# Sample tokens of a streaming trunk layer: two heads on the 128 partitions in both attentions, and two squares of x moved to VectorE

## The chip, the cores and the metric

The kernel runs on one core of one Trainium2 chip. The metric is the time of one execution on the device in microseconds (us), as a median of runs. Matrix products run on TensorE (PE in the profile, its weight loads PEld), elementwise work on VectorE (DVE), ScalarE (ACT) and GpSimd (POOL). SyncE (SP) only issues transfers. All times are in us unless marked ns.

## The reference

One inference step of one layer of a hybrid trunk, for 256 prompt tokens and 64 sample tokens of width 1024:

```python
h = rms_norm(x, p['norm_mix'])
proj = h @ p['w_in']                       # gated delta rule, and queries, latent and rope key of the first attention
o_gdn, s_new = gated_delta_rule(...)       # 4 heads, chunks of 64 tokens
o_mla = block_causal_attention(q * (QK_DIM ** -0.5), k_mla, v_mla, q_pos, k_pos)   # 4 heads, 128 nope + 64 rope
x = x + concatenate([o_gdn, o_mla]) @ p['w_out']

h = rms_norm(x, p['norm_mem'])
sm = einsum('bqhd,bkhd->bhqk', qm, mem_k)  # 4 heads over 256 memory tokens
om = einsum('bhqk,bkhd->bqhd', softmax(sm), mem_v)
x = x + om @ p['w_mo']

h = rms_norm(x, p['norm_ffn'])
x = x + moe_ffn(h, ...)                    # top 4 of 32 experts, w_gu (1024 x 2048), w_down (1024 x 1024) each
```

All of it is in float32. The prompt's first attention is causal by chunks over its own tokens; the 64 sample tokens see 256 cached and 64 own keys, 320 in all.

## The kernel before

Tokens lie in three blocks of rows: two of 128 prompt tokens and one of 64 sample tokens (`TB = 3`, `DEC = 64`). Each engine runs a program of its own; the five are tied together by counting semaphores. The order of the work up to the first attention is a list written out by hand (`CHAIN`). A float32 product is two pairs of weight load and MATMUL in the trace, so counts of such instructions are twice the counts of products. Nearly all products are recorded at L1075 (`mm`), transposes at L1078 (`tr`), ScalarE's activations at L630 (`run`), VectorE's at L1861, L1865, L1866 (`tt`, `ts`).

**Start.** The rows of x are loaded by `ld_x0`, `ld_x1`, `ld_x2`. ScalarE squares the two prompt blocks with an accumulated sum (`x0_sq`, `x1_sq`). VectorE squares the sample rows in two instructions, a product (L1861) and a reduction at L1925 (`x2_sq`). When all three sums stand, ScalarE takes the logarithm and the exponential (`x_logs`, `x_rstd`), VectorE makes diagonals of the result, and TensorE spreads them over the columns before the first projection.

**The two attentions** (`attention`, once in the program of TensorE, ScalarE and VectorE each) go over a list of units, one for each pair of block and head. There are 12: units 0 to 3 are block 0, 4 to 7 block 1, 8 to 11 the sample rows. Step n of TensorE does the scores of unit n, the transposes of the probabilities of unit n-2 and the product with V of unit n-3. VectorE takes the maximum of unit n, scales the probabilities of unit n-1 by the reciprocal of their sum (L2224) and copies out unit n-3 (L2230, `att_o`). ScalarE takes the exponential of unit n and copies the transposes of unit n-2 out of PSUM. A sample unit has 64 rows, thus 64 of 128 partitions. Two banks hold scores, two the transposes, two the results.

Other work is placed between the steps by step number. In the first attention (`mla`), from step 8 on, TensorE adds pieces of the output projection (`GO_AT`: two at step 8, one at each step 9 to 14), and from step 7 on ScalarE scales one eighth of a weight matrix a step (`WQ_AT`). In the second (`mem`), steps 0 to 5 bring x back to rows, `MO_AT` places the four halves of the output projection of blocks 0 and 1 (`mem_out`) at steps 8, 9, 12 and 13, and `X3T_AT` the transposes of block 0 at step 11. `mem_out` waits for the copies of its block's units (`att_o`). ScalarE's square of block 0 (`square_rows(0)`, L1011) is done at step `X3T_AT`, its first bf16 part at `X3T_AT + 3`. Then come the router, the transposes of the other blocks and the projection of the sample rows (`mem_out_pair`, which writes the two halves of the columns to two halves of the partitions).

**Experts.** Each expert takes six tiles of 2 MB, loaded through nine slots. The first nine loads are written out: slots 2 and 3 after the convolution state is stored, 4 and 5 after the first attention, 8, 0, 1, 6 and 7 as their places come free, the last when the router has done its third block. From then on a slot is loaded again (`refill`, L545, or L553 for the last ones) when the tile before it in that slot is used. The loop over experts starts with the gather of expert 0's rows, which needs the router's choice.

Of the kernel before, what the change touches and what calls it, by code (L numbers as in the profile page):

```python
# [88 lines left out]
def trunk_kernel(nc, x_prompt, x_sample, cache_kv_latent, cache_k_rope, state_gdn, state_conv, cache_mem_k,  # L89
# [5 lines left out]
    with ctx:  # L95
# [5 lines left out]
        def sem(name):  # L101
# [9 lines left out]
            "scalar": ["x0_sq", "x1_sq", "x_logs", "x_rstd", "gains_ready", "conv_ready", "bexp_ready", "egc_ready", "kpe_ev"],  # L111
            "vector": ["x2_sq", "diag0", "diag2", "diag1", "rbc_ev", "upad_ready", "state0", "sp_abs", "g_ready", "g2_ready", "gcum_ready", "diff_ready", "dec_ready",
# [16 lines left out]
        ATT = {"mla": 0, "mem": H * TB}  # L129
# [200 lines left out]
        def half(s):  # L330
            return slice(CH * s, CH * s + CH)
# [17 lines left out]
        for b in range(TB):  # L349
            for h in range(H):  # L350
                rows = P if b < 2 else DEC
                qs = slice(b * P, b * P + rows)
                ks = slice(0, (b + 1) * P) if b < 2 else slice(SEQ, NKEY)
                vs = [vk[:, i, h * P:(h + 1) * P] for i in range(b + 1)] if b < 2 else \
                    [vk[:, 2, h * P:(h + 1) * P], vk[:, 3, h * P:(h + 1) * P], vk[0:DEC, 4, h * P:(h + 1) * P]]
                mla_units.append((rows, [(qTn[:, h, qs], kT[:, h, ks]), (qTr[:, h, qs], kpeT[:, ks])],
                                  ks.stop - ks.start, b < 2, vs, hT[:, H + h, qs]))
        for b in range(TB):
            for h in range(H):
                rows = P if b < 2 else DEC  # L360
                qs = slice(b * P, b * P + rows)
                km, vm = (km_p, vm_p) if b < 2 else (km_s, vm_s)
                mem_units.append((rows, [(qmT[:, h, qs], km[:, h, :])], NMEM, False,
                                  [vm[:, i, h * P:(h + 1) * P] for i in range(2)], om[:, h, qs]))
# [218 lines left out]
        def _(pool):  # L583
# [23 lines left out]
            for b in range(TB):  # L607
                if b == 1:
                    pool.wait_ge(sem("att_pv"), ATT["mem"] + H * TB)
# [18 lines left out]
        def _(act):  # L628
# [319 lines left out]
            def attention(tag, units, scale, between):  # L948

                for n in range(len(units) + 3):  # L950
                    between(n)
                    if n < len(units):
                        rows, terms, nkeys, masked, vs, out = units[n]
# [3 lines left out]
                        run(prob[0:rows, n % 2, 0:nkeys], PS[n % 2][0:rows, 0:nkeys], ACT.Exp, scale=scale,  # L957
                            bias=amx[0:rows, n % 2:n % 2 + 1], accum_out=asum[0:rows, n % 2:n % 2 + 1])\
                            .then_inc(sem("att_ex"), 1)
                    if 2 <= n <= len(units) + 1:  # L960
                        rows, terms, nkeys, masked, vs, out = units[n - 2]
# [4 lines left out]
                        if vs[-1].shape[0] == P:  # L966
                            m = run(probT[:, u, 0:len(vs) * P].rearrange("p (t q) -> p t q", q=P)[:, :, 0:rows],
                                    PS[2 + u][:, 0:len(vs) * P].rearrange("p (t q) -> p t q", q=P)[:, :, 0:rows])
                        else:
                            for t, v in enumerate(vs):  # L970
                                m = run(probT[0:v.shape[0], u, t * P:t * P + rows], PS[2 + u][0:v.shape[0], t * P:t * P + rows])
                        m.then_inc(sem("att_pt"), 1)

            def conv_states_and_keys(n):
# [8 lines left out]
                if WQ_AT <= n < WQ_AT + KD:  # L983
                    k = n - WQ_AT
# [40 lines left out]
            def first_block(n):  # L1025
# [4 lines left out]
                if n == X3T_AT + 3:  # L1030
                    part(0, 0)
# [41 lines left out]
        def _(pe):  # L1073
# [429 lines left out]
            def attention(tag, units, between, behind=None):  # L1503


                for n in range(len(units) + 3):
                    between(n)
                    if n < len(units):
                        rows, terms, nkeys, masked, vs, out = units[n]
# [4 lines left out]
                        for t, (q, k) in enumerate(terms):  # L1514
                            m = mm(PS[n % 2][0:rows, 0:nkeys], q, k, t == 0, t == len(terms) - 1)
                        m.then_inc(sem("att_s"), 1)
                    if 2 <= n <= len(units) + 1:
                        rows, terms, nkeys, masked, vs, out = units[n - 2]
# [4 lines left out]
                        for t, v in enumerate(vs):  # L1523
                            kr = v.shape[0]
                            m = tr(PS[2 + u][0:kr, t * P:t * P + rows], prob[0:rows, u, t * P:t * P + kr])
                        m.then_inc(sem("att_tr"), 1)
                    if n >= 3:
                        rows, terms, nkeys, masked, vs, out = units[n - 3]
# [4 lines left out]
                        for t, v in enumerate(vs):  # L1533
                            kr = v.shape[0]
                            m = mm(PS[4 + u][:, 0:rows], v, probT[0:kr, u, t * P:t * P + rows], t == 0, t == len(vs) - 1)
# [6 lines left out]
            def conv_states_and_keys(n):  # L1542
# [19 lines left out]
                for g in {GO_AT: (0, 1)}.get(n, (n - GO_AT + 1,) if n > GO_AT else ()):  # L1562
# [958 lines left out]
```

## Time and profile before

| | |
|---|---|
| median of 3 runs | 1306.26 (1306.18 to 1307.25) |
| time of the profiled execution | 1307.44 |
| its span, first to last instruction | 1305.5 |
| TensorE busy | 1268.4, 97% of the span |
| VectorE busy | 466.9, 36% |
| ScalarE busy | 209.8, 16% |
| GpSimd busy | 21.7, 2% |
| moved by DMA | 439.20 MB, mean 336 GB/s |
| mean granted TensorE clock | 0.997 |

The span is what the trace shows; the time of the same execution is 1.9 longer. The share of busy time is a mean over stages that have different limits, and ends of MATMULs are modelled, so times of products are better taken from start to start. A row of the timeline gives the start, the busy time of a run of like instructions, engine, line, operation, out<-in, and in brackets the idle time of the engine before it and what ended it.

### The profile page before, as it was taken

The numbers are of one execution on the slowest core, as the hardware profiler recorded it, in microseconds if no ns is written. First come the engines' busy times: TensorE is split into PE (matmuls) and PEld (weight loads), VectorE is DVE, ScalarE is ACT, GpSimd is POOL, SyncE is SP. The second block draws the span as 40 slices with busy tenths as digits, with TensorE's granted clock in tenths as the row PEclk, the third lists the DMA queues.
The fourth block names the chain that finished last, engine by engine and source line by source line (L and its number), as shares of the span: only waits on it lengthen the run. The fifth ranks groups of instructions, "written<-read, shape, count | busy, mean of one in ns | idle before, by whom it ended". The sixth has DMA issues, their size and how long they took to land.

```text
span 1305.5 us, 21010 instructions
## 1 busy us (share of the span) xinstructions
PE 1268.4 (97%) x8584; PEld 574.7 (44%) x8584; DVE 466.9 (36%) x988; ACT 209.8 (16%) x565; POOL 21.7 (2%) x35
## 2 busy tenths in 40 slices
PE   7999999999999999999999999999999999999997
PEld 5577655567553333333334333334333333333332
DVE  4455234533663333223333223333222233322233
ACT  2452233730430000000000000000000000000000
POOL 0000011100010000000000000000000000000000
PEclk9999999999989999999999999999999999999999
DMA  9611010771249999999999999999999999999996
GB/s 318 242 65 66 2 30 17 288 285 23 123 194 406 427 430 427 427 431 427 428 430 428 427 430 428 429 429 428 429 428 428 430 427 428 430 428 428 431 427 260
DMA packets 47869, 439.20 MB, mean 336 GB/s; under 512 B 7651, under 2 KB 10313, under 8 KB 23158
## 3 DMA queue, kind: packets, MB, share of 16 engines
q1 hardware_dynamic: 47596, 438.45, 80.6%
q8 instruction: 28, 0.46, 0.1%
q10 hardware_dynamic: 234, 0.20, 0.1%
q14 instruction: 11, 0.09, 0.0%
HBM read 435.30 MB, written 3.33 MB: 336 GB/s over the span
## 4 chain that ended last, share of the span: by engine, by line
PE 78%; DMA 16%; DVE 3%; ACT 1%; issue 1%; POOL 0%; SPq 0%; DVEq 0%; ACTq 0%; POOLq 0%
PE bank L1075 75%; DMA weights<-in_w_gu 15%; PE bank L1078 2%; ACT scaled L630 1%; DMA x<-in_x_sample 0%; POOL stats L591 0%; PE bank L1729 0%; DVE weights L1861 0%; DVE x L2441 0%; DVE x L2297 0%; ACT stream L630 0%; DVE stats L2218 0%; DVE scaled L1861 0%; DVE stream L2348 0%; DVE weights L1972 0%
## 5 line engine op out<-in xcount | busy, mean ns | idle before, releaser
L2441 DVE SCALAR_TENSOR_TENSOR x<-bank,small_weights,x 128x512 f32<-128x512 f32 (+1 forms) x192 | 134.8, 743 | 598.5 <-PE bank L1075 598.5
L1075 PE MATMUL bank<-weights,small_weights 128*64 128x512 f32 (+4 forms) x1456 | 336.1, 588 | 3.7 <-DMA weights<-in_w_gu 3.1
L1075 PEld LDWEIGHTS bank<-weights,small_weights 128*64 128x64 f32 (+1 forms) x1456 | 105.7, 139 | 196.1 <-issue 171.6
L1075 PE MATMUL bank<-weights,scaled 128*64 128x512 f32 x704 | 155.9, 595 | 5.1 <-ACT scaled L630 5.1
L1075 PE MATMUL bank<-scaled,small_weights 64*128 64x512 f32 x384 | 108.1, 640 | 1.4 <-DVE x L2441 0.7
L630 ACT ACTIVATE scaled<-scaled 128x512 f32<-128x512 f32 x32 | 20.1, 629 | 548.2 <-DVE scaled L1865 548.2
L630 ACT ACTIVATE scaled<-bank 128x512 f32<-128x512 f32 (+6 forms) x145 | 54.8, 406 | 323.0 <-PE bank L1075 241.8
L1075 PEld LDWEIGHTS bank<-weights,scaled 128*64 128x64 f32 x704 | 48.7, 137 | 97.1 <-issue 87.8
L1075 PE MATMUL bank<-stream,small_weights 128*64 128x512 f32 (+4 forms) x408 | 88.7, 544 | 1.5 <-DMA stream<-in_w_gu 1.1
L1075 PE MATMUL bank<-small_weights,weights 128*128 128x320 f32 (+3 forms) x320 | 87.6, 424 | 0.0
L1075 PE MATMUL bank<-small_weights 96*64 96x512 bf16 (+2 forms) x408 | 87.0, 499 | 0.0
L1075 PEld LDWEIGHTS bank<-stream 128*128 128x128 bf16 (+1 forms) x2416 | 74.5, 99 | 27.6 <-issue 26.4
L1075 PE MATMUL bank<-stream 128*128 128x64 bf16 (+1 forms) x2416 | 78.7, 195 | 0.3 <-DVE stream L1861 0.3
L1075 PEld LDWEIGHTS bank<-small_weights,weights 128*128 128x128 f32 (+2 forms) x320 | 57.6, 191 | 25.2 <-issue 5.6
L1075 PE MATMUL bank<-weights 64*64 64x64 f32 (+5 forms) x752 | 65.6, 266 | 0.0
L1075 PEld LDWEIGHTS bank<-scaled,small_weights 64*128 64x128 f32 x384 | 29.0, 184 | 79.0 <-issue 75.9
L1075 PEld LDWEIGHTS bank<-small_weights 96*64 96x64 bf16 (+2 forms) x408 | 28.8, 128 | 69.1 <-issue 67.9
L1075 PE MATMUL bank<-small_weights,stream 128*128 128x320 f32 (+4 forms) x212 | 55.5, 412 | 0.4 <-DVE small_weights L2230 0.4
L1075 PEld LDWEIGHTS bank<-stream,small_weights 128*64 128x64 f32 (+1 forms) x408 | 30.9, 143 | 50.6 <-issue 44.4
L1075 PEld LDWEIGHTS bank<-weights 64*64 64x64 f32 (+3 forms) x752 | 38.7, 144 | 23.8 <-issue 21.8
L1075 PEld LDWEIGHTS bank<-small_weights,stream 128*128 128x128 f32 (+1 forms) x212 | 35.2, 187 | 15.0 <-issue 1.9
L1075 PE MATMUL bank<-more_weights,small_weights 128*64 128x512 f32 x176 | 40.2, 598 | 0.6 <-DMA more_weights<-in_w_gu 0.6
(206 smaller groups left out, 899.1 us busy)
## 6 DMA issues: line engine op xcount, KB each, us to landing
weights<-in_w_gu SPq DMA_DIRECT2D x85, 2048.0 KB, 26.9
weights<-in_w_down SPq DMA_DIRECT2D x44, 2048.0 KB, 28.2
stream<-in_w_gu SPq DMA_DIRECT2D x21, 2048.0 KB, 28.0
more_weights<-in_w_gu SPq DMA_DIRECT2D x11, 2048.0 KB, 27.6
small_weights<-in_w_gu SPq DMA_DIRECT2D x11, 2048.0 KB, 26.1
small_weights<-in_w_down SPq DMA_DIRECT2D x10, 2048.0 KB, 28.1
more_weights<-in_w_down SPq DMA_DIRECT2D x10, 2048.0 KB, 28.3
weights<-in_w_in SPq DMA_DIRECT2D x3, 2048.0 KB, 16.3
```

The lines of the kernel that those rows point to most:

```text
L630: return act.activation(out, in_, func, **kw)
L1075: return pe.matmul(out, lhsT, rhs, start=start, stop=stop)
L1078: return pe.transpose(out, in_, ident[0:in_.shape[0], 0:in_.shape[0]])
L2441: dve.scalar_tensor_tensor(xx, PS[bank][0:rows, :], gcur[0:rows, b:b + 1], xx, ALU.mult, ALU.add)\
```

## The change

In both attentions the four sample units become two, each with two heads: head h on partitions 0 to 63 and head h+1 on 64 to 127. Scores of a unit are written by products that alternate between the two halves of the partitions; maximum, exponential, scaling, transposes and copies go over 128 rows; the product with V is done for each head on its own 64 columns. So there are 10 units in each attention (`UNITS`). What is placed by step number is placed anew: the pieces of the output projection at steps 8 to 12, the eighths of the weight matrix two a step at 9 to 12, `MO_AT` at steps 7, 8, 11 and 12, `X3T_AT` at 10, the first bf16 part at `X3T_AT + 2`. Apart from that, VectorE squares the first and the sample block of x, each in one `scalar_tensor_tensor` with an accumulated output; ScalarE squares the second block only.

```diff
-            "scalar": ["x0_sq", "x1_sq", "x_logs", ...
-            "vector": ["x2_sq", "diag0", ...
+            "scalar": ["x1_sq", "x_logs", ...
+            "vector": ["x0_sq", "x2_sq", "diag0", ...
...
-        ATT = {"mla": 0, "mem": H * TB}
+        UNITS = 2 * H + H // 2
+        ATT = {"mla": 0, "mem": UNITS}
...
+        qs, ks = slice(2 * P, T), slice(SEQ, NKEY)
+        for h in range(0, H, 2):
+            two = (h, h + 1)
+            mla_units.append(([[(qTn[:, j, qs], kT[:, j, ks]) for j in two], [(qTr[:, j, qs], kpeT[:, ks]) for j in two]],
+                              ks.stop - ks.start, False,
+                              [[vk[:, 2, j * P:(j + 1) * P], vk[:, 3, j * P:(j + 1) * P], vk[0:DEC, 4, j * P:(j + 1) * P]]
+                               for j in two], hT[:, H + h:H + h + 2, qs]))
+            mem_units.append(([[(qmT[:, j, qs], km_s[:, j, :]) for j in two]], NMEM, False,
+                              [[vm_s[:, i, j * P:(j + 1) * P] for i in range(2)] for j in two], om[:, h:h + 2, qs]))
-        CS_AT, WQ_AT, GO_AT = 2, 7, 8
+        CS_AT = 2
+        WQ_AT = {9: (0, 1), 10: (2, 3), 11: (4, 5), 12: (6, 7)}
+        GO_AT = {8: (0,), 9: (1,), 10: (2, 3), 11: (4, 5), 12: (6, 7)}
-        X2_AT, MO_AT, X3T_AT = 0, {8: (0, 0), 9: (0, 1), 12: (1, 0), 13: (1, 1)}, 11
+        X2_AT, MO_AT, X3T_AT = 0, {7: (0, 0), 8: (0, 1), 11: (1, 0), 12: (1, 1)}, 10
...
-            for b in range(2):
-                act.wait_ge(sem(f"ld_x{b}"), 16)
-                run(x_junk[b], x3[:, b, :], ACT.Square, accum_out=ssq[:, b:b + 1]).then_inc(mark(f"x{b}_sq"), 1)
+            act.wait_ge(sem("ld_x1"), 16)
+            run(x_junk[1], x3[:, 1, :], ACT.Square, accum_out=ssq[:, 1:2]).then_inc(mark("x1_sq"), 1)
...
-                if n == X3T_AT + 3:
+                if n == X3T_AT + 2:
                     part(0, 0)
...
-                        for t, (q, k) in enumerate(terms):
-                            m = mm(PS[n % 2][0:rows, 0:nkeys], q, k, t == 0, t == len(terms) - 1)
+                        for t, sides in enumerate(terms):
+                            for side, (q, k) in enumerate(sides):
+                                m = mm(PS[n % 2][part(side, len(sides)), 0:nkeys], q, k, t == 0, t == len(terms) - 1)
...
-                        for t, v in enumerate(vs):
-                            kr = v.shape[0]
-                            m = mm(PS[4 + u][:, 0:rows], v, probT[0:kr, u, t * P:t * P + rows], t == 0, t == len(vs) - 1)
+                        for side, values in enumerate(vs):
+                            cols = part(side, len(vs))
+                            for t, v in enumerate(values):
+                                m = mm(PS[4 + u][:, cols], v, probT[0:v.shape[0], u, t * P + cols.start:t * P + cols.stop],
+                                       t == 0, t == len(values) - 1)
...
-            dve.wait_ge(sem("ld_x2"), 16)
-            link(tt(x_junk[2][0:DEC, :], x3[0:DEC, 2, :], x3[0:DEC, 2, :], ALU.mult))
-            dve.tensor_reduce(ssq[0:DEC, 2:3], x_junk[2][0:DEC, :], AX, ALU.add).then_inc(mark("x2_sq"), 1)
+            for b in (0, 2):
+                rows = P if b < 2 else DEC
+                dve.wait_ge(sem(f"ld_x{b}"), 16)
+                dve.scalar_tensor_tensor(x_junk[b][0:rows, :], x3[0:rows, b, :], 1.0, x3[0:rows, b, :], ALU.mult, ALU.mult,
+                                         accum_out=ssq[0:rows, b:b + 1]).then_inc(mark(f"x{b}_sq"), 1)
```

## Rows read from the trace of the kernel before

**Rows 1.** The page: GB/s moved in each of forty equal slices.

```profile
GB/s 318 242 65 66 2 30 17 288 285 23 123 194 406 427 430 427 427 431 427 428 430 428 427 430 428 429 429 428 429 428 428 430 427 428 430 428 428 431 427 260
```

**Rows 2.** The page: the chain that ended last, shares by line.

```profile
PE bank L1075 75%; DMA weights<-in_w_gu 15%; PE bank L1078 2%; ACT scaled L630 1%; DMA x<-in_x_sample 0%; POOL stats L591 0%; PE bank L1729 0%; DVE weights L1861 0%; DVE x L2441 0%; DVE x L2297 0%; ACT stream L630 0%; DVE stats L2218 0%; DVE scaled L1861 0%; DVE stream L2348 0%; DVE weights L1972 0%
```

**Rows 3.** The chain in order of time: start, us, what.

```profile
1109.27 40.17 DMA weights<-in_w_gu
...
1153.35 40.13 DMA weights<-in_w_gu
```

**Rows 4.** Timeline of SyncE's queue around expert 0's first tile.

```profile
378.03 0.33 SPq L424 DMA_DIRECT2D small_weights<-in_w_gu  x1
391.65 0.35 SPq L545 DMA_DIRECT2D weights<-in_w_gu  x1
```

**Rows 5.** Windows: length, busy time of each engine, granted clock, DMA share, GB/s.

```profile
390.00:395.00 5.00, 5.00 (x28) 1.60 (x26) 2.37 (x11) 0.00 (x0) 0.00 (x0) 1.00 0.59 180
```

**Rows 6.** Timeline of all engines, the start.

```profile
4.92 4.72 PE L1078 MATMUL bank<-const,x 128*128 128x128 f32 x24 [4.92 <-DMA const<-in_consts]
...
7.94 1.22 DVE L1861 TENSOR_TENSOR scaled<-x 64x1024 f32<-64x1024 f32 x1 [6.01 <-DMA x<-in_x_sample]
...
9.19 1.21 DVE L1925 TENSOR_REDUCE stats<-scaled 64x1 f32<-64x1024 f32 x1
...
10.53 0.30 ACT L630 ACTIVATE stats<-stats,const 128x3 f32<-128x3 f32 x1 [1.98 <-DVE stats L1925]
...
11.52 2.13 PE L1075 MATMUL bank<-more_weights,const 128*128 128x128 f32 x6 [1.82 <-DVE more_weights L1865]
```

**Rows 7.** Groups of VectorE by form, 0 to 80: count, busy, mean ns.

```profile
L1939 DVE SCALAR_TENSOR_TENSOR small_weights<-more_weights,gain_cols 128x320 f32<-128x320 f32 x8 | 3.8, 548 | 0.0
...
L1995 DVE SCALAR_TENSOR_TENSOR stats<-stats 128x10 f32<-128x10 f32 x1 | 0.2, 172 | 0.0
```

**Rows 8.** Timeline, the last steps of the first attention.

```profile
261.40 1.24 PE L1075 MATMUL bank<-small_weights,stream 128*128 128x320 f32 x4
...
262.58 1.43 PE L1075 MATMUL bank<-weights 128*64 128x320 f32 x4
...
263.94 0.44 PE L1078 MATMUL bank<-const,small_weights 128*128 128x128 f32 x2
...
276.25 0.39 PE L1078 MATMUL bank<-const,small_weights 64*128 64x64 f32 x3
...
276.57 1.02 PE L1075 MATMUL bank<-small_weights,weights 128*128 128x64 f32 x6
...
277.52 0.81 PE L1075 MATMUL bank<-small_weights,stream 128*128 128x320 f32 x2
...
279.49 2.93 PE L1075 MATMUL bank<-small_weights,stream 128*128 128x320 f32 x10 [0.41 <-DVE small_weights L2230]
```

**Rows 9.** Timeline, the second attention and the work behind it.

```profile
343.41 0.29 DVE L2230 COPY stream<-bank 128x128 f32<-128x128 f32 x1
...
354.25 0.65 PE L1075 MATMUL bank<-stream,small_weights 128*64 128x256 f32 x2
...
356.56 1.05 ACT L1011 ACTIVATE scaled<-x 128x1024 f32<-128x1024 f32 x1
...
358.39 0.20 PEld L1078 LDWEIGHTS bank<-const,small_weights 64*128 64x128 f32 x2 [0.42 <-DVE small_weights L1865]
...
363.63 3.65 PE L1075 MATMUL bank<-weights,stream 128*128 128x512 f32 x8
...
367.51 1.92 PE L1075 MATMUL bank<-stream,small_weights 128*128 128x32 f32 x16
...
370.27 3.65 PE L1075 MATMUL bank<-weights,stream 128*64 128x512 f32 x16
```

**Rows 10.** Windows: TensorE's busy time and its granted clock.

```profile
330.00:340.00 10.00, 7.79 (x51) 5.89 (x50) 9.39 (x30) 5.50 (x20) 0.00 (x0) 1.00 0.66 279
380.00:381.00 1.00, 0.00 (x0) 0.00 (x0) 0.93 (x5) 0.00 (x0) 0.57 (x1) 0.50 1.04 442
```

More of the change, by code:

```diff
@@ L348, in trunk_kernel @@
         mla_units, mem_units = [], []
-        for b in range(TB):
+        for b in range(2):
             for h in range(H):
[L351 to L364, printed above, removed]
-        CS_AT, WQ_AT, GO_AT = 2, 7, 8
+                qs, ks = slice(b * P, (b + 1) * P), slice(0, (b + 1) * P)
@@ new lines, in trunk_kernel @@
+                mla_units.append(([[(qTn[:, h, qs], kT[:, h, ks])], [(qTr[:, h, qs], kpeT[:, ks])]], ks.stop, True,
+                                  [[vk[:, i, h * P:(h + 1) * P] for i in range(b + 1)]], hT[:, H + h:H + h + 1, qs]))
+                mem_units.append(([[(qmT[:, h, qs], km_p[:, h, :])]], NMEM, False,
+                                  [[vm_p[:, i, h * P:(h + 1) * P] for i in range(2)]], om[:, h:h + 1, qs]))
+        qs, ks = slice(2 * P, T), slice(SEQ, NKEY)
[7 more added lines that the diff above has]
+                              [[vm_s[:, i, j * P:(j + 1) * P] for i in range(2)] for j in two], om[:, h:h + 2, qs]))
@@ L952, in attention @@
                     if n < len(units):
-                        rows, terms, nkeys, masked, vs, out = units[n]
+                        terms, nkeys, masked, vs, out = units[n]
                         act.wait_ge(sem("att_mx"), ATT[tag] + n + 1)
@@ L956, in attention @@
                             act.wait_ge(sem("att_tr"), ATT[tag] + n - 1)
-                        run(prob[0:rows, n % 2, 0:nkeys], PS[n % 2][0:rows, 0:nkeys], ACT.Exp, scale=scale,
-                            bias=amx[0:rows, n % 2:n % 2 + 1], accum_out=asum[0:rows, n % 2:n % 2 + 1])\
+                        run(prob[:, n % 2, 0:nkeys], PS[n % 2][:, 0:nkeys], ACT.Exp, scale=scale,
+                            bias=amx[:, n % 2:n % 2 + 1], accum_out=asum[:, n % 2:n % 2 + 1])\
                             .then_inc(sem("att_ex"), 1)
                     if 2 <= n <= len(units) + 1:
-                        rows, terms, nkeys, masked, vs, out = units[n - 2]
+                        terms, nkeys, masked, vs, out = units[n - 2]
                         u = n % 2
@@ L965, in attention @@
                             act.wait_ge(sem("att_pv"), ATT[tag] + n - 3)
[L966 to L969, printed above, removed]
-                            for t, v in enumerate(vs):
-                                m = run(probT[0:v.shape[0], u, t * P:t * P + rows], PS[2 + u][0:v.shape[0], t * P:t * P + rows])
+                        whole = nkeys // P * P
+                        m = run(probT[:, u, 0:whole], PS[2 + u][:, 0:whole])
+                        if nkeys > whole:
+                            m = run(probT[0:nkeys - whole, u, whole:whole + P], PS[2 + u][0:nkeys - whole, whole:whole + P])
                         m.then_inc(sem("att_pt"), 1)
@@ L982, in conv_states_and_keys @@
                     run(cs_out[:, i // 3, 512 * (i % 3):512 * (i % 3) + 512], PS[6 + i % 2][0:3, :]).then_inc(sem("cs_ev"), 1)
-                if WQ_AT <= n < WQ_AT + KD:
-                    k = n - WQ_AT
+                for k in WQ_AT.get(n, ()):
                     if k == 0:
@@ L1503, in attention, with part @@
             def attention(tag, units, between, behind=None):
+                def part(side, sides):
+                    return slice(0, P) if sides == 1 else half(side)
                 for n in range(len(units) + 3):
@@ L1508, in attention @@
                     if n < len(units):
-                        rows, terms, nkeys, masked, vs, out = units[n]
+                        terms, nkeys, masked, vs, out = units[n]
                         if tag == "mem" and n < H:
@@ L1522, in attention @@
                             pe.wait_ge(sem("att_pt"), ATT[tag] + n - 3)
-                        for t, v in enumerate(vs):
+                        for t, v in enumerate(vs[0]):
                             kr = v.shape[0]
-                            m = tr(PS[2 + u][0:kr, t * P:t * P + rows], prob[0:rows, u, t * P:t * P + kr])
+                            m = tr(PS[2 + u][0:kr, t * P:(t + 1) * P], prob[:, u, t * P:t * P + kr])
                         m.then_inc(sem("att_tr"), 1)
                     if n >= 3:
-                        rows, terms, nkeys, masked, vs, out = units[n - 3]
+                        terms, nkeys, masked, vs, out = units[n - 3]
                         u = (n - 3) % 2
@@ L1561, in conv_states_and_keys @@
                     m.then_inc(sem("cs_tr"), 1)
-                for g in {GO_AT: (0, 1)}.get(n, (n - GO_AT + 1,) if n > GO_AT else ()):
+                for g in GO_AT.get(n, ()):
                     k, i = g // 4, g % 4
@@ L2209, in attention @@
                     if n < len(units):
-                        rows, terms, nkeys, masked, vs, out = units[n]
+                        terms, nkeys, masked, vs, out = units[n]
                         dve.wait_ge(sem("att_s"), ATT[tag] + n + 1)
@@ L2213, in attention @@
                             dve.wait_ge(sem("att_ex"), ATT[tag] + n - 1)
[L2214 removed]
+                        sc = PS[n % 2][:, 0:nkeys]
                         if masked:
                             link(tt(sc[:, nkeys - P:nkeys], sc[:, nkeys - P:nkeys], amask, ALU.add))
[L2217 removed]
+                        a = amx[:, n % 2:n % 2 + 1]
                         link(dve.tensor_reduce(a, sc, AX, ALU.max))
```

28 lines of the change are left out of this document (13 added, 15 removed).

## The prediction

> **What bounds the kernel now.** I read the page first. From the thirteenth of forty slices to the last but one the core's loads move a steady 427 or so GB/s (406 in the first of them) [rows 1]. The chain that ended last puts 75% on matrix products but 15% on loads of the expert weights [rows 2]. The chain in order of time says where: one link is a weight load of 40.17 us, the next one begins 44.08 us after it [rows 3]. A slot is used again nine tiles later, so this is nine tiles in 44.08 us, 4.90 us a tile. An expert takes six tiles, 29.4 us of loading. So the end is set by the weight stream, not by TensorE, however busy that looks.
>
> When does the stream start? Nine tiles are loaded ahead; the last of them is issued at 378.03 after the router of the sample block, and the first refill at 391.65, when expert 0 has used its first tile [rows 4]. Between 390 and 395 the DMA share is only 0.59 [rows 5], so the early tiles are in and the stream waits for TensorE there. Then 192 - 9 = 183 tiles follow: 183 x 4.90 = 896.7, ending near 1288, and the last expert and the stores fill the rest up to 1305.5. So whatever brings expert 0 forward brings the first refill and the end forward by the same amount, and what only speeds TensorE up later is worth nothing. The change lies wholly before 391.65. I price three stretches there.
>
> **1. Squares of x.** Before: VectorE multiplies the sample rows (7.94, 1.22 us, when their load has landed), then reduces (9.19, 1.21); ScalarE can take the logarithm at 10.53, and TensorE's next work follows at 11.52 [rows 6]. The change merges the two into one instruction with an accumulated output. No such instruction is in the trace. Nearest: the same operation without it takes 548 ns for 320 columns and 172 ns for 10 [rows 7], so 1.21 ns a column, 1.41 us for 1024; as a plain product it would be 1.22. For the accumulator I add 0.1. The sum is ready at 7.94 + 1.5 = 9.45 in place of 10.4: 0.9 us gained. Bounds: 1.2 at the rate of the plain product; nothing if accumulating costs as much as the reduction did. The first rows' square moves onto VectorE ahead of it: their load had landed by 4.92, when TensorE transposes them [rows 6], so it runs from about 5 to 6.5 (7.4 at the dear bound) and is hidden by the wait for the sample rows. If that cover were gone it would cost its own 1.5. ScalarE drops one square and is idle before the logarithm anyway. TensorE then goes on from 11.52 to expert 0 without a wait on a weight load, so I let the 0.9 pass through.
>
> The Trainium skill, Vector Engine (DVE) Microarchitecture Reference, section "Points that are easy to get wrong", says that this operation with two sources in SBUF that aren't bf16 halves throughput. The rows speak against it: the plain product's 1.22 [rows 6] is 1.03 ns a column over a start of 0.17; at that rate 320 columns take 0.50, at half of it 0.83, and 0.548 was measured [rows 7]. By the rule the merged instruction would be no shorter than the two it replaces. It is rival B.
>
> **2. First attention.** A step of TensorE is, in order of issue: pieces of the output projection, scores of unit n, transposes of unit n-2, products with V of unit n-3. From the first such step, whose pieces begin at 261.40, to the next phase at 279.49 [rows 8] TensorE has hardly a gap.
> - Scores of a sample unit: 262.58 to 263.94, 1.36 us for two products (nope, rope), 64 columns of the array wide [rows 8]; four units, 5.44. After: two units, each with two pairs that alternate array halves. A pair's price comes from the sample block's output projection: 16 instructions that alternate halves take 3.65, as much as 8 on the full width [rows 9]. So a pair costs like one product: two instructions of 512 columns at 0.43 each (3.65 for eight, less a modelled end), for 320 columns 0.53. The 1.36 of a unit is four such instructions, 1.07, and a rest of 0.15 per product for the change of tile shape; with it a pair is 0.7. Four pairs: 2.8. Gain 2.6. If halves do not overlap in such short runs, gain 0; without the 0.15, 3.3.
> - Transposes: three take 0.32 (276.25 to 276.57) [rows 8]. Twelve become six of twice the rows, 0.11 each: gain 0.6.
> - Products with V: 12 before and 12 after, 64 columns each, 0.95 per three [rows 8]: 0.
> - Output projection pieces: eight before and eight after. Two in a row are busy for 1.24, 0.62 each, one alone for 0.81 [rows 8]; of the difference I take under half, 0.08, as more than a modelled end. Six stood alone, two will: gain 0.3.
> Sum 3.5, two steps fewer. ScalarE scales eight weight pieces in the last four steps, two at a time, 0.7 each. The exponential of unit 9 comes behind two of them and is done near 267.6, while its transposes are due near 270; the last scaling ends near 273.5, while the last product with V starts at 273.7. Both fit, with little to spare at the second; past that point each microsecond is lost. VectorE does half the sample units and is not late.
>
> **3. Second attention.** Here the change moves work. The output projection of block 0 comes one step earlier, before the scores of unit 7. It needs the copy of unit 3, which ends at 343.41 + 0.29 = 343.70 [rows 9]; nothing before it is changed. TensorE used to do the scores of unit 7 and part of the transposes of unit 5 meanwhile; now it stands 1.1 us. Counting from 343.76 to the router at 367.51 [rows 9]:
> - scores 4 x 0.58 (a unit's 0.65 less a modelled tail of 0.07, as 1.43 stands against 1.36 in the first attention; [rows 8, 9]) become two pairs of 0.60: -1.1
> - transposes, 4 x 0.27 to 2 x 0.27: -0.55
> - the wait of 0.4 ahead of unit 10's transposes [rows 9] goes with the unit: -0.4; two changes of tile shape less: -0.25
> - moved behind the wait, scores 7 and transposes 5: +0.75
> - new: ScalarE squares block 0 (1.05 plus the accumulator read) ahead of the copy of unit 8's transposes. Before, a 0.26 copy stood in front of the square; now unit 8's products with V wait for the copy behind it: +0.9
> Gain 0.65, I take 0.6. Bounds: 1.6 if neither wait bites, -0.6 if the pairs don't overlap. What follows the router (second transposes, block 2's projection, top-4, gather) moves along; GpSimd's clearing starts earlier, off the path.
>
> **Sum.** 0.9 + 3.5 + 0.6 = 5.0. The profiled execution took 1307.44 (span 1305.5); on it, 1302.4. It lies 1.2 above the median of 1306.26; on the median, 1301.3.
>
> The granted clock is a term of unknown sign. It is 0.50 of full (1.2 GHz) at 380 to 381 [rows 10], after the thin products of the router, and comes back during expert 0's gather. With the work shifted by 5 us the two flanks can lie up to some us elsewhere against it; a gather wholly at full speed would be about 1 us shorter, a longer low stretch about 1 longer.
>
> **The rivals.**
> - A, as summed: 1301.3. Chance 0.58.
> - B, the start gives nothing (the accumulated form is as slow as the two), or the two new waits in the second attention eat its gain: 1301.3 + 0.9 = 1302.2, or 1301.9, or both 1302.8. For: no row of the form; two waits argued from single rows. Chance 0.21, of it 0.08 for the halved rate.
> - C, array halves overlap in long runs only: the scores give back 2.6 and 1.1, 1305.0. For: each run is just four instructions between changes of shape. Against: if they overlapped only late in a run, the run of 16 would be longer than that of 8 by about a half product, and both take 3.65 [rows 9]. 0.09.
> - D, no effect: the stream is held by something other than expert 0, 1306.3. Against: the share of 0.59 before it. 0.04.
> - E, slower: the 1.1 us stop before block 0's projection, with the thin work around it, lets the clock fall to 0.50 for the two projections behind it, 7 us of work that would take 14: 1301.3 + 7 = 1308. It decides from 5 us of full-speed work done at half. Against: between 330 and 340 TensorE was busy for only 7.79 of 10 and kept 1.00 [rows 10]. 0.03.
> - F, both waits vanish and the clock helps: 1299.3. 0.05.
>
> The Trainium skill, TensorE: Matmul & The Clock Gate, section "HAM oscillation", tells that waits inside TensorE's work can throttle it again and again; this speaks for E, and in the stretch of 7.79 the trace does not agree.
>
> **Numbers.** 0.2% is 2.6 us, about what a measurement can tell from no change, so the border is 1303.6. Faster: A, B, F and a little of C, 0.86; same: C and D, 0.11; slower 0.03. The range goes from F to half way into C, 1299.3 to 1304.0, leaving out most of C, D and E.
>
> **What would show it.** The logarithm at 9.5 to 9.6; an unbroken series in the first attention, whose next phase begins near 275.1 (279.49 - 0.9 - 3.5); alternating 64-wide products for two heads in 0.7 a pair; a TensorE gap near 342 and another before unit 8's products with V; the router near 362.5; the first refill near 386.6; still 44.1 us from weight-load link to link at the end. Wrong would be: a start still at 10.5; pairs of 1.4; a first refill that comes 5 us earlier with an end that doesn't; a second low-clock stretch.

## The result, and the profile after

The changed kernel takes 1299.74 (median of 5 runs, 1298.11 to 1300.08), the kernel before beside it 1306.32 (1306.18 to 1307.64). The ratio is 0.994, interval 0.9928 to 0.9952: faster by 6.3 to 9.4 with 7.8 in the middle (0.006 x 1306.3), where 5.0 was forecast and the range ended at 1299.3, 7.0 below the time before. So the median, 6.6 faster, lies 0.4 inside the range, and the middle of the paired ratio lies outside it. The profiled execution took 1298.11 (span 1296.3, mean clock 0.993).

From the profile page of the changed kernel, GB/s in forty slices (before: [rows 1]) and the chain that ended last (before: [rows 2]):

```profile
GB/s 319 246 66 67 2 30 17 297 280 90 58 254 428 428 427 429 429 428 429 429 428 428 429 428 429 429 427 428 428 429 428 428 429 429 428 429 429 429 429 264
...
PE bank L1074 75%; DMA weights<-in_w_gu 15%; PE bank L1077 2%; ACT scaled L633 1%; DMA x<-in_x_sample 0%; POOL stats L594 0%; PE bank L1734 0%; DVE weights L1866 0%; DVE x L2449 0%; DVE x L2305 0%; DVE stats L2225 0%; ACT stream L633 0%; DVE x L1866 0%; ACT scaled L1010 0%; DVE weights L1979 0%
```

The chain in order of time (before: [rows 3]), and SyncE's queue around the first refill (before: [rows 4]):

```profile
1100.41 40.18 DMA weights<-in_w_gu
1144.51 40.14 DMA weights<-in_w_gu
1188.54 40.17 DMA weights<-in_w_gu
```

```profile
369.32 0.33 SPq L427 DMA_DIRECT2D small_weights<-in_w_gu  x1
382.65 0.35 SPq L548 DMA_DIRECT2D weights<-in_w_gu  x1
```

The stream is as it was: links still follow each other by 44.1 (1144.51 - 1100.41). The first refill is issued at 382.65 in place of 391.65, 9.00 earlier; from it to the end of the span are 913.65 where there were 913.83. So the span of this execution is shorter by what came off before the refill. The three stretches that the change edits:

The start, all engines (before: [rows 6]):

```profile
4.75 1.22 DVE L1931 SCALAR_TENSOR_TENSOR weights<-x 128x1024 f32<-128x1024 f32 x1 [2.82 <-DMA x<-in_x_prompt]
5.90 0.08 DVE L1931 DVE_READ_ACCUMULATOR weights<-x 128x1 f32 x1
...
7.67 1.22 DVE L1931 SCALAR_TENSOR_TENSOR scaled<-x 64x1024 f32<-64x1024 f32 x1 [1.69 <-DMA x<-in_x_sample]
8.82 0.07 DVE L1931 DVE_READ_ACCUMULATOR scaled<-x 64x1 f32 x1
9.02 0.30 ACT L633 ACTIVATE stats<-stats,const 128x3 f32<-128x3 f32 x1 [1.31 <-DVE scaled L1931]
```

From the start of VectorE's work on the sample rows to the logarithm are 1.35 us, before 10.53 - 7.94 = 2.59. The accumulated form costs what the plain product costs, 1.22, and a read of 0.07. The other 0.27 by which the logarithm is earlier is the load of these rows, which landed sooner in this execution.

The last steps of the first attention, TensorE (before: [rows 8]):

```profile
257.42 0.70 PE L1074 MATMUL bank<-small_weights,stream 128*128 128x320 f32 x2
258.06 1.45 PE L1074 MATMUL bank<-weights 128*64 128x320 f32 x8
259.43 0.44 PE L1077 MATMUL bank<-const,small_weights 128*128 128x128 f32 x2
...
262.88 1.24 PE L1074 MATMUL bank<-small_weights,stream 128*128 128x320 f32 x4
263.96 0.49 PE L1077 MATMUL bank<-const,small_weights 128*128 128x128 f32 x3
264.29 0.61 PE L1074 MATMUL bank<-small_weights,weights 128*128 128x128 f32 x4
264.74 1.24 PE L1074 MATMUL bank<-small_weights,stream 128*128 128x320 f32 x4
...
266.14 1.87 PE L1074 MATMUL bank<-small_weights,weights 128*128 128x64 f32 x12
267.94 1.34 PE L1074 MATMUL bank<-small_weights,stream 128*128 128x320 f32 x4
269.12 1.87 PE L1074 MATMUL bank<-small_weights,weights 128*128 128x64 f32 x12
```

Eight instructions that alternate between the halves of the array take 259.43 - 258.06 = 1.37, as long as the four of one head did (1.36): two heads for one. There are no gaps, so the scalings of the weight matrix fit beside it.

The second attention, TensorE and the square on ScalarE (before: [rows 9]):

```profile
335.72 3.70 PE L1074 MATMUL bank<-weights,stream 128*128 128x512 f32 x8 [0.84 <-DVE stream L2237]
...
343.88 0.65 PE L1074 MATMUL bank<-stream,small_weights 128*64 128x256 f32 x4
...
347.73 1.05 ACT L1010 ACTIVATE scaled<-x 128x1024 f32<-128x1024 f32 x1
...
349.20 1.10 PE L1074 MATMUL bank<-small_weights,stream 128*128 128x64 f32 x8 [0.38 <-ACT small_weights L633]
350.15 3.65 PE L1074 MATMUL bank<-weights,stream 128*128 128x512 f32 x8
...
357.96 1.87 PE L1074 MATMUL bank<-stream,small_weights 128*128 128x32 f32 x16
```

Both waits that were forecast are there: 0.84 for the copy of unit 3 and 0.38 for ScalarE's copy behind the square.

**Lengths between marks.** The span of one execution doesn't tell these gains apart from the clock, so I read each profile between marks of its timelines: the logarithm; ScalarE's square of the memory rows (`sq`); SyncE's load of `in_w_mq`; its store of the convolution state; the MEMSET of x that opens the phase behind the first attention; the load that waits for the third block's x (`x3`); the router's first product; the first refill; the end. Two stretches are left out: `sq` to `in_w_mq` takes 205.27 to 205.29 in all fourteen profiles, and the phase to `x3` 45.18 or 45.19 in all but two, which are named below. The kernels of the later rows are described with the experiments; "again" is another execution of the same kernel.

```
                       log   log-sq  w_mq-conv conv-phase x3-router router-refill refill-end  span
before                 10.53  29.62   15.58     18.61      42.71     24.14         913.83    1305.5
before, again 1        10.43  29.41   18.77     18.61      42.72     24.15         913.78    1308.3
before, again 2        10.46  28.51   18.79     18.60      42.73     24.16         913.77    1307.5
after                   9.02  27.16   15.57     14.56      41.19     24.69         913.65    1296.3
after, again 1          9.38  28.50   17.15     14.57      41.19     24.35         913.92    1299.5
after, again 2          9.29  28.27   15.57     14.57      41.19     24.54         913.72    1297.6
start_only              9.53  28.52   20.35     21.37      42.72     24.53         914.13    1313.4
sample_square_only      9.23  28.26   15.58     21.34      42.73     24.55         913.79    1307.7
first_only             10.79  28.38   15.58     14.56      42.72     24.00         914.12    1300.6
second_only            10.38  28.42   17.15     18.61      41.20     25.00         914.23    1305.5
heads_in_turn           9.25  27.17   15.58     17.25      41.19     24.77         914.21    1299.9
projection_later        9.44  28.38   15.57     14.56      40.89     24.73         913.93    1298.0
square_behind           9.09  28.38   15.58     14.56      41.07     24.65         914.16    1298.0
square_and_projection   9.37  28.37   15.58     14.56      41.48     24.46         913.92    1298.2
```

The two attentions repeat within 0.02: 4.05 us come off the first (18.61 to 14.56) and 1.52 off the second (42.71 to 41.19). The other columns differ between executions of one kernel.

### The profile page after: what moved, and what is told of

Read it like the earlier page. It is cut to its first block, busy times and chain, and to the rows that moved or that the text cites. A ratio compares the mean times of both kernels' runs of the same rounds, so it can differ in the third digit from the quotient of the medians.

```text
span 1296.3 us, 20932 instructions
## 1 busy us (share of the span) xinstructions
PE 1261.5 (97%) x8574; PEld 573.7 (44%) x8574; DVE 462.6 (36%) x970; ACT 205.4 (16%) x545; POOL 22.1 (2%) x35
## 4 chain that ended last, share of the span: by engine, by line
PE 77%; DMA 16%; DVE 3%; ACT 2%; issue 1%; POOL 1%; SPq 0%; DVEq 0%; ACTq 0%; POOLq 0%
PE bank L1074 75%; DMA weights<-in_w_gu 15%; PE bank L1077 2%; ACT scaled L633 1%; DMA x<-in_x_sample 0%; POOL stats L594 0%; PE bank L1734 0%; DVE weights L1866 0%; DVE x L2449 0%; DVE x L2305 0%; DVE stats L2225 0%; ACT stream L633 0%; DVE x L1866 0%; ACT scaled L1010 0%; DVE weights L1979 0%
## 5 line engine op out<-in xcount | busy, mean ns | idle before, releaser
L1074 PE MATMUL bank<-weights 64*64 64x64 f32 (+5 forms) x752 | 62.7, 266 | 0.0
## 6 DMA issues: line engine op xcount, KB each, us to landing
stream<-in_w_gu SPq DMA_DIRECT2D x21, 2048.0 KB, 28.1
more_weights<-in_w_down SPq DMA_DIRECT2D x10, 2048.0 KB, 28.4
```

What stands on the lines that cost most here:

```text
L1074: return pe.matmul(out, lhsT, rhs, start=start, stop=stop)
```

## The experiments

**One part at a time.** Three kernels take one part of the change each, into the kernel before. `start_only` has the squares alone. `first_only` pairs the heads in the first attention and places `GO_AT` and `WQ_AT` as the change does; `second_only` pairs them in the second, with the new `MO_AT` and `X3T_AT`. The attention that isn't changed runs over units of one head, in the old order:

```diff
# first_only
+        for two in (((0, 1), (2, 3))):          # first attention
...
+        for two in (((0,), (1,), (2,), (3,))):  # second attention
```

> Before plus only the squares' change (first and sample block squared on VectorE with accumulated output). In the profile after, this start was 3.97 us earlier by the first convolution, of which the instruction itself explains 1.24, an earlier landing of the sample rows 0.27; in the other 2.46 TensorE does the same products in less time. Theory T (the clock's rise falls differently in each execution, whatever the change): the logarithm about 9.0 to 9.3, time 1.2 us below before within the scatter of runs, and TensorE's speed in the first 20 us differs between profiles of kernels with the same start. Theory S (the shorter pause of TensorE before the spreading products lets the clock rise earlier, every time): 3.7 us below before. The forecast's term: 0.9.

> Before plus only the first attention's four sample units as two, with the output projection's pieces placed as in the change; start and second attention as before. Expected from the profile after: the stretch from the first sample unit's step to the next phase 4.05 us shorter, the time 4.0 us below before. The forecast's term: 3.5. If the gains of the change were not additive (weight stream held elsewhere) less than 3.

> Before plus only the second attention's sample units as two, with the output projection of blocks 0 and 1 one step earlier. Expected from the profile after: the router 1.5 us earlier, time 1.5 us below before, up to 0.7 us less or more by where the low clock of TensorE lies at expert 0's gather. The forecast's term: 0.6.

Measured in 5 rounds, with 1308.59 for the kernel before (1305.02 to 1316.06): `start_only` 1305.83, ratio 0.998 (0.9966 to 0.9993); `first_only` 1304.86, 0.9977 (0.996 to 0.9995); `second_only` 1308.5, 1.0001 (0.9983 to 1.0019). The intervals are as wide as the parts, so the times tell only that the first two are faster and not how much. The lengths tell more: `first_only` takes 14.56 over the first attention and 42.72 over the second, `second_only` 18.61 and 41.20. Each part does in its own stretch, to 0.01, what the whole does there, and nothing in the other. They are additive up to the router. `start_only` has its logarithm 1.35 after the start of VectorE's work on the sample rows (9.53 - 8.18), like the changed kernel.

The profiles show one reason why the times scatter: TensorE's granted clock falls in places where it doesn't in other executions. Windows of `start_only`: two stretches at 0.50, the full clock between them.

```profile
251.00:261.00 10.00, 10.00 (x32) 5.50 (x29) 3.94 (x17) 3.84 (x13) 0.00 (x0) 0.50 0.66 244
261.00:273.00 12.00, 12.00 (x59) 6.46 (x59) 6.29 (x26) 6.49 (x18) 0.00 (x0) 0.99 0.64 208
278.00:288.00 10.00, 9.59 (x27) 6.60 (x28) 1.59 (x4) 2.73 (x6) 0.00 (x0) 0.51 0.31 93
```

The first makes `w_mq` to the store of the convolution state 20.35 in place of 15.58, 4.8 more. The second, also in `sample_square_only` (0.50 from 273 to 283), lengthens the first attention by 2.7 to 2.8 (21.34 and 21.37 for 18.61) and the phase behind it to 46.94 and 46.96 for 45.18. In this profile of `start_only` the three lengthenings, 4.77, 2.76 and 1.76, add up to 9.3. Its execution took 1315.2, the longest of the twelve; less 9.3 that is 1305.9, next to their median of 1305.83.

**The first rows' square left on ScalarE.** `sample_square_only` merges the sample rows' product and reduction and moves nothing.

```diff
-            link(tt(x_junk[2][0:DEC, :], x3[0:DEC, 2, :], x3[0:DEC, 2, :], ALU.mult))
-            dve.tensor_reduce(ssq[0:DEC, 2:3], x_junk[2][0:DEC, :], AX, ALU.add).then_inc(mark("x2_sq"), 1)
+            dve.scalar_tensor_tensor(x_junk[b][0:rows, :], x3[0:rows, b, :], 1.0, x3[0:rows, b, :], ALU.mult, ALU.mult,
+                                     accum_out=ssq[0:rows, b:b + 1]).then_inc(mark(f"x{b}_sq"), 1)
```

> Before plus only the accumulated form for the sample rows; both prompt blocks' squares stay on ScalarE. ScalarE ends its two squares near 8.6 to 8.8, the sample rows' sum stands near 8.9 to 9.2, so the logarithm starts at 9.0 to 9.3 as in the whole change: moving the first block's square to VectorE is worth 0 to 0.2 us. If the move itself matters the logarithm comes at 9.8 or later. Time 1.2 us below before by theory T, 3.7 by theory S.

Measured: 1306.54, 0.9994 (0.9978 to 1.0009), which tells nothing. Its timeline does, all engines at the start:

```profile
7.50 1.04 ACT L630 ACTIVATE weights<-x 128x1024 f32<-128x1024 f32 x1
7.89 1.22 DVE L1926 SCALAR_TENSOR_TENSOR scaled<-x 64x1024 f32<-64x1024 f32 x1 [5.95 <-DMA x<-in_x_sample]
8.44 0.19 ACT L630 ACTIVATION_READ_ACCUMULATOR weights<-x 128x1 f32 x1
9.04 0.07 DVE L1926 DVE_READ_ACCUMULATOR scaled<-x 64x1 f32 x1
9.23 0.30 ACT L630 ACTIVATE stats<-stats,const 128x3 f32<-128x3 f32 x1 [0.60 <-DVE scaled L1926]
```

ScalarE has both its squares done near 8.6, VectorE its one at 9.1; the logarithm comes 1.34 after the start of VectorE's instruction, as in the changed kernel (1.35). The merging is the whole gain. Moving the first rows' square is worth nothing, because ScalarE had room for it.

**Do array halves overlap in short runs?** `heads_in_turn` is the changed kernel with the scores of the first attention written head after head. The second attention has one product a head there, so its order stays.

```diff
-                        for t, sides in enumerate(terms):
-                            for side, (q, k) in enumerate(sides):
+                        for side in range(len(terms[0])):
+                            for t, sides in enumerate(terms):
+                                q, k = sides[side]
```

> The changed kernel with the scores of a two-head unit written head after head (nope and rope of the first, then nope and rope of the second) in place of alternating array halves product by product. Theory H (the gain in the first attention comes from products on the two halves running at the same time, which needs them side by side): a unit's scores take 4 x 0.68 = 2.7 in place of 1.37 us, the last steps of the first attention 2.7 us longer (14.56 to 17.3), time 2.7 above the changed kernel. Rival (the gain comes from half the steps and waits, not from overlap): no change. The second attention has one product a head and stays.

Measured: 1302.6 in 3 rounds, 0.9958 (0.9944 to 0.9972), with 1307.77 for the kernel before. TensorE's timeline:

```profile
258.32 2.79 PE L1074 MATMUL bank<-weights 128*64 128x320 f32 x8
261.04 0.44 PE L1077 MATMUL bank<-const,small_weights 128*128 128x128 f32 x2
```

The same eight instructions take 2.72 in turn and 1.37 alternating; the stretch is 17.25 for 14.56, 2.69 more for two units. The time is 2.5 to 2.9 more than that of the next three kernels, which differ from the changed one only by small moves and were measured in the same set (1299.68 to 1300.14). The overlap of the halves is shown, and it is two thirds of what the first attention gains.

**The two waits of the second attention.** `projection_later` puts block 0's output projection a step later, where the copy of unit 3 is ready. `square_behind` keeps the changed kernel's steps, but lets ScalarE copy unit 8's transposes before it squares block 0. `square_and_projection` does both.

```diff
# projection_later
-        X2_AT, MO_AT, X3T_AT = 0, {7: (0, 0), 8: (0, 1), 11: (1, 0), 12: (1, 1)}, 10
+        X2_AT, MO_AT, X3T_AT = 0, {8: (0, 0), 9: (0, 1), 11: (1, 0), 12: (1, 1)}, 10
# square_behind, in attention, behind the copies of step n; the call in first_block goes
+                    if behind is not None:
+                        behind(n)
-            attention("mem", mem_units, HD ** -0.5, first_block)
+            attention("mem", mem_units, HD ** -0.5, first_block, square_behind)
```

> The changed kernel with the output projection of block 0 at steps 8 and 9 of the second attention in place of 7 and 8. TensorE's wait of 0.84 us for the copy of unit 3 should go. Theory W (the wait is lost time): the stretch up to the router shortens by 0.5 to 0.8 us. Rival V (it only turns into another wait, since the transposes of block 0 at step 10 then come right behind the second half and its addition on VectorE): 0 to 0.3.

> The changed kernel with ScalarE's square of block 0 behind, not ahead of, the copy of unit 8's transposes. The products with V of unit 8 waited 0.4 to 0.5 us for that copy: they should start right after the transposes of unit 9, the router 0.4 us earlier. If the square's chain (GpSimd's root, VectorE's scaling) were the later one, nothing.

> Both edits together. If the waits are independent: the router 0.9 to 1.2 us earlier than in the changed kernel; if the wait moves to the transposes of block 0: 0.4 to 0.6. Time below the changed kernel by as much, little against the scatter that TensorE's clock brings.

Measured in 5 rounds: 1299.86, 0.9933 (0.9919 to 0.9947); 1300.14, 0.9938 (0.9924 to 0.9952); 1299.68, 0.9936 (0.9921 to 0.9951). None differs from the changed kernel (0.994, 0.9928 to 0.9952). In the lengths from `x3` to the router they are -0.30, -0.12 and +0.29 against 41.19. Forecast were -0.5 to -0.8 or 0 to -0.3 for the first, -0.4 or nothing for the second, and -0.9 to -1.2 or -0.4 to -0.6 for both. The first came out as its second theory had it, the second between its two, and both together missed with the sign wrong. Rows of TensorE say why so little; first of `projection_later`, then of `square_behind`:

```profile
349.11 0.66 PE L1077 MATMUL bank<-const,x 128*128 128x128 f32 x4 [0.71 <-DVE x L1866]
```

```profile
349.95 1.00 PE L1078 MATMUL bank<-small_weights,stream 128*128 128x64 f32 x8
351.31 1.96 PE L1078 MATMUL bank<-weights,stream 128*128 128x512 f32 x4 [0.35 <-DVE stream L2241]
```

With the projection later, TensorE doesn't stop before it, but block 0's x is ready later too and its transposes wait 0.71. With the square behind, unit 8's products with V start at once, and then the next projection waits 0.35 for VectorE's copy of unit 7. Each wait that was taken away came back as another one: the 0.84 for VectorE's copy as 0.71 for VectorE's addition to x, the 0.38 for ScalarE as 0.35 for VectorE. With both edits TensorE waits 0.71 for block 0's x and then 0.51 for a copy of ScalarE, and the stretch gets longer. The three moves change it by 0.3 at most.

**Is the stretch behind the logarithm part of the change?** Between the logarithm and the square of the memory rows, where the change edits nothing, the profile after is 2.46 ahead (27.16 for 29.62). Two more executions of each kernel were profiled:

> The kernel before once more, unchanged. Theory T: the length of TensorE's early half-clock stretch differs from execution to execution for one and the same kernel, so from the logarithm to the square of the memory rows this execution may take 28.3 or so in place of the 29.62 of the profile before, with all later stages alike within 0.02 as long as the clock is full; such a length would be 1 to 1.4 apart between two executions of one kernel. Theory G: the changed start shortens the half-clock stretch itself; then the kernel before repeats 29.6 within 0.2, and the kernel after repeats 27.2.

> The changed kernel once more. Theory T: from the logarithm to the square of the memory rows either 27.2 or 28.4. Theory G: 27.2 again. Both: convolution state to the next phase 14.56, third block's x to the router 41.19, first refill to the end 913.7 to 914.2.

> A third look at the kernel before. Theory T: a value among 28.4 and 29.6 in the stage behind the logarithm, not the same in all three looks. Theory G: 29.6.

> A third look at the changed kernel. Theory T: 27.2 or 28.4 in the stage behind the logarithm, not the same in all three looks. Theory G: 27.2.

Times of the single runs: 1310.24 and 1309.3 for the kernel before, 1301.43 and 1299.44 for the changed one. The stretch is 29.62, 29.41, 28.51 before and 27.16, 28.50, 28.27 after: neither kernel repeats itself. It follows TensorE's clock. The profile after, its windows (the clock is third from the end), and then TensorE's timeline up to 20, the row of the first projection:

```profile
12.00:16.00 4.00, 3.82 (x10) 2.37 (x10) 3.83 (x10) 1.04 (x4) 0.00 (x0) 0.57 1.03 394
16.00:20.00 4.00, 4.00 (x17) 2.81 (x16) 1.05 (x5) 0.50 (x2) 0.00 (x0) 1.00 1.06 394
```

```profile
12.30 8.12 PE L1074 MATMUL bank<-small_weights,weights 128*128 128x320 f32 x23 [0.18 <-ACT more_weights L633]
```

The same two views of the second repetition of the changed kernel:

```profile
17.00:20.00 3.00, 3.00 (x12) 2.09 (x11) 0.33 (x1) 0.04 (x1) 0.00 (x0) 1.00 1.07 397
```

```profile
13.73 6.46 PE L1074 MATMUL bank<-small_weights,weights 128*128 128x320 f32 x17
```

Where the granted clock is 0.50, these instructions of 320 columns start 0.53 apart, where it is 1.00 0.27. In the second of these executions the trace has no record of the clock before 17.0, and windows ahead of that print 1.00 all the same; there the spacing tells. It changes from 0.53 to 0.27 at 15.9 in the first of them, 6.9 behind the logarithm, and at 17.0 in the second, 7.7 behind it. In the other repetition of the changed kernel it changes 9.1 behind the logarithm, in the three profiles of the kernel before 10.5, 10.0 and 9.2. In all six the stretch is the longer the later the full clock comes.

So up to 1.3 of the 2.46 (28.50 against 27.16) is chance between executions of one kernel. The repetitions also show the later low stretch: TensorE's windows of `before, again 1` and of `after, again 1`, the clock third from the end.

```profile
252.00:259.00 7.00, 7.00 (x24) 4.13 (x24) 2.73 (x12) 3.42 (x11) 0.00 (x0) 0.54 0.96 352
```

```profile
250.00:254.00 4.00, 4.00 (x15) 2.25 (x15) 1.30 (x6) 2.16 (x7) 0.00 (x0) 0.58 0.80 261
```

It costs 3.2 there (18.77 for 15.58) and 1.6 here (17.15), with the same instructions on TensorE. It isn't the change's doing: the kernel before has it in two of three profiles.

## Why the prediction was right or wrong

**Right: the bound.** From the first refill to the end fourteen profiles, with first refills from 382.65 to 399.25, take 913.65 to 914.23. The stream of weights sets the end, and expert 0's first tile sets the stream (rival D is out).

**Right: the mechanisms.** All three parts gain, in their own stretches; pairs cost one product (rival C is out, `heads_in_turn`); both waits of the second attention are real; no second low-clock stretch came there. Rival E's stop of 0.84 before block 0's projection was followed by products at full clock. The stretch of 7.79 busy us that the prediction held against E had waits of 1.38 at most, so it spoke of short waits alone; this stop is shorter still. The window of the changed kernel that begins before it:

```profile
330.00:340.00 10.00, 8.94 (x43) 5.62 (x42) 5.57 (x21) 3.08 (x12) 0.00 (x0) 1.00 0.01 2
```

**Wrong: the sizes of the terms, each too small.** The sum of work is 1.24 + 4.05 + 1.52 = 6.8, not 0.9 + 3.5 + 0.6 = 5.0. The step that failed worst is the charge for the second new wait of the second attention; after it come the output pieces of the first attention and the price of the accumulated form.
- Squares: 1.24 for 0.9. I priced the accumulated form at 1.5, from 1.21 ns a column between the rows of 10 and 320 columns [rows 7]; it measured 1.22 and 0.07, and from 320 to 1024 columns it is 0.95 ns a column. Rival B's halved rate is out with it. The rule of the Trainium skill, Vector Engine (DVE) Microarchitecture Reference, "Points that are easy to get wrong", that two sources in SBUF that aren't bf16 halve the throughput, does not agree with this trace, if it means half the rate of the plain product, as the prediction took it: 1024 float32 columns of two such sources take 1.22, what the plain product takes.
- First attention: 4.05 for 3.5. Scores 2.7 for 2.6 and transposes 0.6 as worked out. The output pieces were the miss: from start to start they are 0.64, 0.64, 1.08, 1.08 and 1.18, in all 4.62 for the 5.21 of before, 0.6 gained for 0.3. I took 0.08 for each of the four pieces that no longer stand alone, from a gap of 0.19 between busy times; it was 0.15 each (0.59 over four). Products with V gave some 0.1, twelve instructions in 1.80 (267.94 - 266.14) for twice the 0.95 of [rows 8].
- Second attention: 1.52 for 0.6, the term that was furthest off. I charged 0.9 for unit 8's products with V behind the square; the wait was 0.38, since TensorE had block 0's transposes and unit 7's products to do meanwhile. That is 0.5 of the 0.9. The other 0.4 lies in pieces of 0.1 to 0.2 that I had not listed: a wait of 0.21 ahead of transposes that is filled now, transposes of x 0.87 for 0.97.

The range was too narrow below for the same reason: only rival F left both waits out, at 0.05, and the bound for the second attention (1.6) was nearly reached without the waits vanishing. That bound was also summed wrongly. Without either wait the prediction's own terms give 1.1 + 0.55 + 0.4 + 0.25 = 2.3; 1.6 leaves the 0.75 of the first wait in. By these terms F is 1301.3 - 0.9 - 0.75 - 1 = 1298.65, and not 1299.3, and the range would have begun there. I took middle values for three unknown prices in a row and let none of them err to the cheap side together.

**The clock term was looked for in one place, and it is in three.** The gather, router to refill, got longer, 24.69, 24.35 and 24.54 for 24.14 to 24.16, which takes back 0.2 to 0.55. The low clock behind the router [rows 10] is there in the changed kernel too. In the profile after it lasts from 367.5 to 377.8, in the one before from 379.4 to 386.2; a longer low stretch was the prediction's dearer case for this term.

```profile
372.00:373.00 1.00, 1.00 (x6) 0.74 (x8) 1.00 (x2) 0.00 (x0) 0.00 (x0) 0.50 1.11 475
```

The prediction put nothing on the start and on the stretch near 251, and they scatter more: by 1.4 (28.52 for 27.16, both with the new start) and by 4.8. On the mean of three profiles each, the first refill is 393.30 before and 384.06 after, 9.2 apart: 1.24 + 4.04 + 1.52 - 0.38 = 6.4 that repeat, 1.2 behind the logarithm and 1.6 near 251. The 6.6 between the medians fits the first sum alone; the ratio's interval, 6.3 to 9.4, reaches to both. How much of its middle, 7.8, is clock stays open.

**Open.** Whether the earlier logarithm makes the low stretch at the start shorter on average. The five profiles that have the old start take 28.4 to 29.6 behind the logarithm (mean 28.9), the nine with the new one 27.2 to 28.5 (mean 28.1), and they overlap; that is no proof. What makes the clock fall near 251 and between 273 and 278 in some executions is open as well.

**The marks that were forecast.** The logarithm is at 9.02 to 9.38 (9.5 to 9.6), the phase behind the first attention at 271.58, 272.99 and 274.88 (275.1), the router at 357.96 to 361.26 (362.5), the first refill at 382.65 to 385.61 (386.6). All are early, by the terms above and the clock.

## What to carry to other kernels

Where a stream of loads sets the end, price only what stands ahead of its first refill, and measure it there: the length from refill to end is a constant against which each microsecond before it can be counted. Heads with 64 rows can share the array if products for the two halves alternate; written one after the other they share nothing. Prefer lengths between marks, in several executions, to one span: a part of 1.5 us was measured to 0.02 that way, while the ratio of its times over 5 rounds was 1.0001 (0.9983 to 1.0019).

## What the runs showed of the hardware

- An accumulated output on VectorE's `scalar_tensor_tensor` costs a read of 0.07 to 0.08 us; ScalarE's costs 0.19.
- TensorE's granted clock fell to 0.50 amid float32 products in some executions and not in others. In `start_only` TensorE was busy 8.75 of the 10 us before 251, and 10.00 of the 10 us before 278, when it fell again. A stretch near 251 cost 1.6, 3.2 or 4.8 us. That the medians of the kernel before differ by 2.3 from one set of runs to another (1306.3 to 1308.6) fits it. But sets also ran on different chips (1308.59 on one, 1307.77 on another), so the cause isn't shown.
- Two products of 320 float32 columns for each of two heads, 64 wide, took 1.37 us when they alternated between the halves of the array, and 2.72 in turn; those of one head alone took 1.36.
